# Gathering the experts' rows already transposed, two pairs at once from a three-part bfloat16 copy of h

## The reference, cut to what matters

```
def hier_moe(x, w_group, w_expert, w_gate, w_up, w_down):
    ...
    top_p, top_i = lax.top_k(jax.nn.softmax(e_logits, axis=-1), MOE_TOP_K)
    ...
    rows = xpad[row_tok].reshape(n_blocks, MOE_BLOCK, d)

    def expert_block(args):
        xb, e = args
        h = jax.nn.silu(xb @ w_gate[e]) * (xb @ w_up[e])
        return h @ w_down[e]

    yb = lax.map(expert_block, (rows, block_expert)).reshape(P, d)
    out = jax.ops.segment_sum(yb * row_w[:, None], row_tok, num_segments=T + 1)[:T]
```

## Time and profile before

| | us |
|---|---|
| median of 3 runs | 2106.32 |
| lowest, highest | 2104.14, 2111.51 |
| the profiled execution, its own time | 2105.5 |
| span of the profiled execution | 2103.7 |
| PE busy in the span | 2004.5 |
| DVE busy | 671.4 |
| ACT busy | 446.4 |

### The profile page before, as it was taken

The page is one execution under the profiler, slowest core; times in us unless marked ns, Lnnn a source line. Parts: engine busy times, 40 slices in busy tenths (PEclk is TensorE's granted clock), DMA queues, the critical chain, the costliest instruction groups (busy, mean ns, idle before and its releaser), DMA issues.

```text
span 2103.7 us, 20350 instructions
## 1 busy us (share of the span) xinstructions
PE 2004.5 (95%) x8337; PEld 1058.7 (50%) x8337; DVE 671.4 (32%) x1469; ACT 446.4 (21%) x961; POOL 61.0 (3%) x55
## 2 busy tenths in 40 slices
PE   9999999999999989978999999997779999989999
PEld 8888643333333334444333333332445656438873
DVE  3555331111111122224111111112224545424994
ACT  2222201011110101231110111101124433204770
POOL 0000000000000000000000000000000000000110
PEclk9999999999999999989999999999779999999999
DMA  9333338999999957214999999995411213231412
GB/s 387 126 121 121 117 144 354 423 426 428 428 427 428 428 227 326 80 40 180 387 424 426 426 427 428 428 428 230 168 49 40 121 40 120 81 120 40 200 57 84
DMA packets 40206, 522.46 MB, mean 248 GB/s; under 512 B 4384, under 2 KB 6944, under 8 KB 8368
## 3 DMA queue, kind: packets, MB, share of 16 engines
q1 hardware_dynamic: 38240, 514.52, 59.2%
q10 hardware_dynamic: 1872, 6.61, 0.8%
HBM read 520.06 MB, written 1.05 MB: 248 GB/s over the span
## 4 chain that ended last, share of the span: by engine, by line
PE 90%; DVE 5%; ACT 3%; DMA 1%; issue 1%; POOL 1%; SPq 0%; ACTq 0%; DVEq 0%
PE ps L194 33%; PE ps L602 21%; PE ps L624 11%; PE ps L634 6%; PE ps L573 5%; PE ps L589 1%; PE ps L1143 1%; PE ps L1014 1%; PE ps L982 1%; PE ps L966 1%; PE ps L869 1%; PE ps L987 1%; PE ps L509 1%; PE ps L610 1%; PE ps L522 1%
## 5 line engine op out<-in xcount | busy, mean ns | idle before, releaser
L602 PE MATMUL ps<-ring,work 128*64 128x512 f32 x2048 | 445.0, 592 | 0.7 <-issue 0.7
L194 PE MATMUL ps<-xT,ring 128*128 128x272 f32 (+1 forms) x1280 | 300.6, 394 | 2.1 <-DMA ring<-in_w_xz 1.8
L602 PEld LDWEIGHTS ps<-ring,work 128*64 128x64 f32 x2048 | 148.7, 137 | 290.3 <-issue 290.3
L194 PEld LDWEIGHTS ps<-xT,ring 128*128 128x128 f32 x1280 | 245.7, 193 | 48.7 <-issue 4.5
L624 PE MATMUL ps<-ring,work 128*64 128x512 f32 x1024 | 226.8, 595 | 1.4 <-ACT work L1321 1.4
L194 PE MATMUL ps<-ring,xT 128*128 128x256 f32 (+2 forms) x672 | 209.7, 471 | 3.8 <-DMA ring<-in_w_qkv 2.3
L194 PE MATMUL ps<-ring,big 128*128 128x512 f32 x448 | 199.9, 603 | 4.3 <-ACT ring L1558 1.8
L1813 DVE TENSOR_TENSOR work<-work,ps 128x512 f32<-128x512 f32 x32 | 22.0, 687 | 524.3 <-PE ps L602 524.3
L194 PEld LDWEIGHTS ps<-ring,xT 128*128 128x128 f32 x672 | 128.6, 194 | 80.0 <-issue 68.0
L194 PEld LDWEIGHTS ps<-ring,big 128*128 128x128 f32 x448 | 85.2, 193 | 110.5 <-issue 108.1
L624 PEld LDWEIGHTS ps<-ring,work 128*64 128x64 f32 x1024 | 70.7, 137 | 134.8 <-issue 127.9
(11 more groups left out here) (330 smaller groups left out, 1763.0 us busy)
## 6 DMA issues: line engine op xcount, KB each, us to landing
ring<-in_wg SPq DMA_DIRECT2D x64, 2048.0 KB, 14.5
ring<-in_wu SPq DMA_DIRECT2D x64, 2048.0 KB, 17.4
ring<-in_wd SPq DMA_DIRECT2D x64, 2048.0 KB, 13.2
ring<-in_w_odd SPq DMA_DIRECT2D x8, 2048.0 KB, 7.9
ring<-in_w_xz SPq DMA_DIRECT2D x7, 2048.0 KB, 17.5
ring<-in_w_qkv SPq DMA_DIRECT2D x6, 2048.0 KB, 19.5
ring<-in_w_bc SPq DMA_DIRECT2D x4, 2048.0 KB, 15.1
ring<-in_ssm_out SPq DMA_DIRECT2D x4, 2048.0 KB, 7.9
```

Source lines behind the costliest of these rows:

```text
L194: i = e.matmul(bout, lhs(k), rhs(k), start=start and k == ks[0], stop=stop and k == ks[-1])
L602: last = e.matmul(b[64 * j:64 * j + 64, :], xgT[:, p % 2, k, 64 * j:64 * j + 64], w[j][:, k, :], start=k == 0, stop=k == 7)
```

## The change

- The gather swaps its operands: h is now the stationary operand and S the moving one, so that the product comes out transposed. turn_x, `xgs` and its two copies are gone.
- Pairs 0 and 1 are gathered so in float32, each by itself: 16 matmuls of 128 columns.
- Pairs 2 to 15 are gathered two pairs at once. `hb` holds h as three bfloat16 parts: the rounded value, the rounded rest, and the rest of that. Sb, the 0/1 matrix for two pairs, is 256 wide and bfloat16. A piece s (2 to 15) is half of the 1024 rows of xgT for two pairs: 24 bfloat16 matmuls of 128 weight columns by 256, summed in float32. One piece is done for each pair, two pairs ahead; pair 1 has two pieces (s = 2 and 3).
- The three parts are made once in each layer: two casts on ScalarE and two subtractions on VectorE, of 2048 elements in each partition.
- In the loop the gather moves from before turn_h to after it. SW is turned in a function of its own (`tensor_turn_w`) just before down.
- The banks are fixed: ps0 for gate and the turned SW, ps1 for up and turn_h, ps2 and ps3 for gather and down. Down waits for the copies of the gather just before it; up waits for the copy of hT of the pair before; gate waits for the copy of the turned SW.

The core of the diff (the copies in `scalar_gathered` and `vector_gathered` write PSUM to xgT, one of each for a piece):

```diff
+        Sb = m(512).bitcast(BF16).rearrange("p (i t n) -> p i t n", i=2, t=2)
+        xgT, sg, hs, hT = m(2, 8, 256), m(512), m(512), m(4, 128)
+        rest = xgT[:, 1].rearrange("p k n -> p (k n)").rearrange("p (t n) -> p t n", t=2)
+        ys, hb = area(big, 0, (1024,)), big[:, 1024:4096].bitcast(BF16).rearrange("p (i t n) -> p i t n", i=3, t=2)
...
+        gate_b, up_b, swt_b, th_b, row_b = ps[0], ps[1], ps[0], ps[1], ps[2:4]
...
+        def tensor_gather(e, l, s):
+
+
+            e.wait_ge(*listed(l, s if s < 2 else s // 2 * 2))
+            if s == 2:
+                e.wait_ge(*hb1_in(l))
+                e.wait_ge(*hb2_in(l))
+                e.wait_ge(*hb3_in(l))
+            for i in range(2):
+                b = row_b[i]
+                if s:
+                    e.wait_ge(*(xg1 if i else xg0)(l, 0 if s == 1 else 2 if s == 3 else s - 1))
+                if s > 1:
+                    e.wait_ge(*(ys1 if i else ys0)(l, 0 if s < 4 else s - 3))
+                for k in range(4 if s < 2 else 2):
+                    if s < 2:
+                        o = b[:, k * 128:(k + 1) * 128]
+                        for t in range(2):
+                            last = e.matmul(o, h[:, t, (4 * i + k) * 128:(4 * i + k + 1) * 128], S[:, s, t, :],
+                                            start=t == 0, stop=t == 1)
+                    else:
+                        o, c = b[:, k * 256:(k + 1) * 256], (4 * (s % 2) + 2 * i + k) * 128
+                        for t, j in each(range(2), range(3)):
+                            last = e.matmul(o, hb[:, j, t, c:c + 128], Sb[:, s // 2 % 2, t, :],
+                                            start=t + j == 0, stop=t + j == 3)
+                last.then_inc(*gat_mm.up(l, s, i))
+
...
-        def tensor_turn_x(e, l, p):
-            for n in range(2):
-                e.wait_ge(*(xg0(l, p) if n == 0 else xg1(l, p)))
-                b = moe_bank(p - 1, TX0 + n)
-                for k in range(4):
-                    last = e.transpose(b[:, k * 128:(k + 1) * 128], xgs[:, (4 * n + k) * 128:(4 * n + k + 1) * 128],
-                                       ident)
-                last.then_inc(*tx_mm.up(l, p, n))
-
...
+            for s in ((p,) if p < 2 else (p // 2 * 2, p // 2 * 2 + 1)):
+                e.wait_ge(*xg0(l, s))
+                e.wait_ge(*xg1(l, s))
+            x = xgT[:, p // 2 % 2, :, 128 * (p % 2):128 * (p % 2) + 128]
+            for name, b, done in (("mg", gate_b, gate_mm), ("mu", up_b, up_mm)):
+                if name == "mg":
+                    e.wait_ge(*swt_in(l, p))
+                else:
+                    e.wait_ge(*(hT_in(l, p - 1) if p else flagged(l)))
...
-            if p + 1 < NE // 2:
-                e.wait_ge(*swt_in(l, p + 1))
...
+                b, s = row_b[n], 1 if p == 0 else min(p + 2, NE // 2 - 1)
+                e.wait_ge(*(xg1 if n else xg0)(l, s))
+                if p:
+                    e.wait_ge(*(ys1 if n else ys0)(l, p - 1))
...
             tensor_warm(e, ps[2], 6)
             tensor_gather(e, l, 0)
-            tensor_turn_x(e, l, 0)
+            e.matmul(ps[1][:, 0:32], ones[:, :], mk[:, 0, :], start=True, stop=False)
+            e.matmul(ps[1][:, 0:32], ones[:, :], mk[:, 1, :], start=False, stop=True).then_inc(*cnt_mm.up(l))
             e.wait_ge(*ranked(l))
-            e.matmul(b[:, 0:32], ones[:, :], mk[:, 0, :], start=True, stop=False)
-            e.matmul(b[:, 0:32], ones[:, :], mk[:, 1, :], start=False, stop=True).then_inc(*cnt_mm.up(l))
+            tensor_turn_w(e, l, 0)
             for p in P16:
                 tensor_hidden(e, l, p)
                 if p:
                     tensor_spread(e, l, p - 1)
+                if p == 1:
+                    tensor_gather(e, l, 2)
+                tensor_turn_h(e, l, p)
+                if p + 2 < NE // 2:
+                    tensor_gather(e, l, 1 if p == 0 else p + 2)
                 if p + 1 < NE // 2:
-                    tensor_gather(e, l, p + 1)
-                tensor_turn_h(e, l, p)
-                if p + 1 < NE // 2:
-                    tensor_turn_x(e, l, p + 1)
+                    tensor_turn_w(e, l, p + 1)
                 tensor_down(e, l, p)
...
+            e.copy(hb[:, 0], h[:, 0:2, :]).then_inc(*hb1_in.up(l))
             scalar_gathered(e, l, 0)
-            scalar_turned_x(e, l, 0)
+            scalar_turned_w(e, l, 0)
+            e.wait_ge(*rest_in(l))
+            e.copy(hb[:, 1], rest).then_inc(*hb2_in.up(l))
             for p in P16:
...
+        def vector_lists(e, l, s):
+
+            iota64 = R("iota")[:, 0:64]
+            if s > 4:
+                e.wait_ge(*gat_mm(l, s - 3, 1))
+            for j, t in each(range(2 if s < 2 else 4), range(2)):
+                x = 2 * s + j
+                o = S[:, s, t, 64 * j:64 * j + 64] if s < 2 else Sb[:, s // 2 % 2, t, 64 * j:64 * j + 64]
+                e.tensor_scalar(o, iota64, rk[:, t, x:x + 1], None, ALU.is_equal).then_inc(
+                    *(listed.up(l, s) if t and j == (1 if s < 2 else 3) else vs.up()))
+
...
+            vector_lists(e, l, 1)
+            vector_weights(e, l, 1)
+            e.wait_ge(*hb1_in(l))
+            e.tensor_tensor(rest, h[:, 0:2, :], hb[:, 0], ALU.subtract).then_inc(*rest_in.up(l))
+            vector_lists(e, l, 2)
+            e.wait_ge(*hb2_in(l))
+            e.wait_ge(*rest_in(l))
+            e.tensor_tensor(hb[:, 2], rest, hb[:, 1], ALU.subtract).then_inc(*hb3_in.up(l))
...
+                if p == 1:
+                    vector_gathered(e, l, 2)
+                if p + 2 < NE // 2:
+                    vector_gathered(e, l, 1 if p == 0 else p + 2)
+                    vector_weights(e, l, p + 2)
+                if p % 2 and p + 3 < NE // 2:
+                    vector_lists(e, l, p + 3)
```

More of the change, by code:

```diff
@@ L563, in tensor_router @@
             tensor_warm(e, idle, 20)
-        def tensor_gather(e, l, p):
-            e.wait_ge(*listed(l, p))
-            for n in range(2):
[L568 to L575, removed]
+        def tensor_gather(e, l, s):
[22 more added lines that the diff above has]
+                last.then_inc(*gat_mm.up(l, s, i))
@@ L576, in tensor_gather, with tensor_turn_w @@
+        def tensor_turn_w(e, l, p):
+            e.wait_ge(*weighted(l, p))
             if p:
                 e.wait_ge(*silu_in(l, p - 1))
-            e.wait_ge(*weighted(l, p))
-            b = moe_bank(p - 1, SWTB)
             for t in range(2):
-                last = e.transpose(b[:, t * 128:(t + 1) * 128], SW[:, p % 2, t, :], ident)
+                last = e.transpose(swt_b[:, t * 128:(t + 1) * 128], SW[:, p % 2, t, :], ident)
             last.then_inc(*swt_mm.up(l, p))
-        def tensor_turn_x(e, l, p):
-            for n in range(2):
-                e.wait_ge(*(xg0(l, p) if n == 0 else xg1(l, p)))
-                b = moe_bank(p - 1, TX0 + n)
-                for k in range(4):
-                    last = e.transpose(b[:, k * 128:(k + 1) * 128], xgs[:, (4 * n + k) * 128:(4 * n + k + 1) * 128],
-                                       ident)
-                last.then_inc(*tx_mm.up(l, p, n))
@@ L601, in tensor_hidden @@
                     for j in range(2):
-                        last = e.matmul(b[64 * j:64 * j + 64, :], xgT[:, p % 2, k, 64 * j:64 * j + 64], w[j][:, k, :],
+                        last = e.matmul(b[64 * j:64 * j + 64, :], x[:, k, 64 * j:64 * j + 64], w[j][:, k, :],
                                         start=k == 0, stop=k == 7)
@@ L1288, in scalar_mixed, with gathered, scalar_gathered, scalar_turned_w @@
             e.activation(s4[:, :, 4], s4[:, :, 3], ACT.Exp).then_inc(*e_exp.up(l))
[L1290 to L1294, removed]
+        def gathered(s, i):
+            if s < 2:
+                return xgT[:, 0, 4 * i:4 * i + 4, 128 * s:128 * s + 128]
+            k = 4 * (s % 2) + 2 * i
+            return xgT[:, s // 2 % 2, k:k + 2, :]
+        def scalar_gathered(e, l, s):
+            e.wait_ge(*gat_mm(l, s, 1))
+            e.copy(gathered(s, 1), row_b[1][:, :].rearrange("p (k n) -> p k n", k=4 if s < 2 else 2)
+                   ).then_inc(*xg1.up(l, s))
+        def scalar_turned_w(e, l, p):
             e.wait_ge(*swt_mm(l, p))
@@ L1297, in scalar_gathered @@
                 e.wait_ge(*spr_mm(l, p - 2))
[L1298 to L1304, removed]
+            e.copy(SWT[:, p % 2, :, :], swt_b[:, 0:256].rearrange("p (t n) -> p t n", t=2)).then_inc(*swt_in.up(l, p))
         def scalar_moe(e, l):
@@ L1320, in scalar_moe @@
                     e.wait_ge(*dn_mm(l, p - 1, 1))
[L1321 removed]
+                e.copy(hT, th_b[:, :].rearrange("p (f s) -> p f s", f=4)).then_inc(*hT_in.up(l, p))
+                if p + 2 < NE // 2:
+                    scalar_gathered(e, l, 1 if p == 0 else p + 2)
                 if p + 1 < NE // 2:
[L1323 removed]
+                    scalar_turned_w(e, l, p + 1)
                 e.wait_ge(*dn_mm(l, p, 1))
@@ L1326, in scalar_moe @@
                     e.wait_ge(*spr_mm(l, p - 1))
```

(2 more changed lines are left out.)

66 lines of the change are left out of this document (21 added, 45 removed).

## The result

The changed kernel takes 2096.19 us (median of five runs, 2093.76 to 2098.46) against 2106.32 before. The ratio is 0.995, with an interval of 0.9934 to 0.9967. The forecast was 2096.5. The profiled execution was the longest of the five, 2098.46, with a span of 2096.3, 7.4 less than before's span.

A forecast was written before the change was run, and what follows sets the result against it. PE and the expert loads were both taken as full, with loads setting the layer's end after the change. 2105.5 - 4.1 - 5.3 = 2096.1, plus 0.8 for the median, 2096.9; 2096.5 was taken, range 2088 to 2104.

The forecast's parts named there:

- The loads need as long for a pair as PE does: Mixture layers before the change: six 2 MiB loads take 29.5 us a pair, PE 29.34.
- The rival in which PE's saving counts in full: Both layers: PE's whole saving, 48 us, reaches the time, giving 2057; chance 0.03.
- The piece's cost, 0.114 a matmul, and a steady pair of 27.7: Gather on PE: 24 matmuls at 0.114 us make 2.75 a piece, taking a pair from 29.34 to 27.7.
- The slower rival: Gather pieces: weight loads stand in line with matmuls, a piece takes 5.3 us; down 11.4 late, 2128; chance 0.08.
- PE alone: down of pair 15 at 748.0: Layer 0's end without load waits: last down starts at 748.0, 24 us before 771.85.
- Waits of 1.8 us a pair from pair 7 on: Later pairs: PE waits 1.8 us a pair for mu, and the period goes to 29.5.
- The waits that cost nothing: Within a pair and at layer start: added waits for copies, products and h's parts stay hidden, costing 0.
- The chain of loads: Loads up to the last mu: 0.3 earlier start, plus md of pair 1's hole closed, 0.5 (layer 0) and 1.7 (layer 1).
- From the last mu to down, 11.74: Pair 15: after mu lands, up takes 6.92 us, then 4.82 more until down starts.
- the rival of the falling clock: Pair 15's new wait: clock falls to half, up loses 6.9 us a layer; 2110, or 2103 in one layer; chance 0.10.
- The sum, -4.1 and -5.3: Last down starts 4.1 us earlier in layer 0 and 5.3 in layer 1, passed on whole to the kernel's time.
- The end hardly depends on the unknown pace: Layer's end: loads set it unless each of 336 piece matmuls takes 0.059 us more, 0.173.

The follow-up runs named there:

- experiment 1: Kernel before the change, loading only the first half of each expert matrix in layer 1: 2106.3 us, ratio 1.0005.
- experiment 2: Changed kernel, loading only the first half of each expert matrix in layer 1: 2077.09 us, ratio 0.9862.
- experiment 8: Changed kernel with every matmul of a piece done twice (24 more per piece): 2130.89 us, ratio 1.0118.
- experiment 3: Changed kernel with all pairs gathered transposed in float32, one pair at a time, still two pairs ahead, no bfloat16 parts: 2099.56 us, ratio 0.9971.
- experiment 7: Changed kernel with 12 more bfloat16 matmuls in each piece: 2103.09 us, ratio 0.9986.
- experiment 4: Changed kernel with spread of the pair before moved between gate and up, and the gather's piece put before turn_h: 2094.47 us, ratio 0.9942.
- experiment 10: Changed kernel with every gather transposed in float32 without bfloat16 parts, one pair ahead instead of two: 2095.56 us, ratio 0.9946.
- experiment 9: Changed kernel with 12 more matmuls in each piece, only from piece 4 on: 2098.58 us, ratio 0.9963.

## Why the prediction was right, step by step

- **"The loads need as long for a pair as PE does", and "the loads forbid" PE's saving.** Shown by experiments 1, 2 and 8 and by the DMA share of 1.00. The rival in which PE's saving counts in full (2057) fell.
- **The piece's cost, 0.114 a matmul, and a steady pair of 27.7.** Measured 0.109 and 27.66. The slower rival, in which the weight loads (98 ns) stand in line, fell. By the Trainium skill (TensorE: Matmul & The Clock Gate, The mechanism) a load of weights overlaps matmuls only in another group of rows, and by the page's formulas a piece would then be an estimated 5.2 us; the trace has 2.62, and the trace decides. The same section also lets a load into a background weight buffer go ahead, which the trace does not contradict; no run here can tell whether that is what happens.
- **PE alone: down of pair 15 at 748.0.** Counted from the start of gate, forecast there at 314.6, that is 433.4; experiment 2 has 432.5.
- **Waits of 1.8 us a pair from pair 7 on.** In layer 0 there are nine, 15.8 us in all, the first at 518.88. Most are 1.5, two are 2.7, and the period is 29.4.
- **The waits that cost nothing.** So it was: the parts of h were done at 323.3, forecast before 325, and no wait of over 0.9 us but for loads stands in either layer.
- **Gate 0.3 earlier.** From the first gather to gate it was 5.08 for 5.75: 0.67. The transposes of SW lie beneath the first copies more than was allowed for.
- **The chain of loads.** This term was sized too small. The last mu was to land 0.8 earlier in layer 0 and 2.0 in layer 1. From the first gather it landed at 444.5 (733.07 + 22.1 - 310.72) against 447.7 before, and at 444.6 (1410.39 + 22.1 - 987.86) against 447.7: 3.2 and 3.1 earlier. Little of it is the start: the first waiting load was issued 0.67 earlier, but landed only 0.3 earlier in layer 0 and 0.2 in layer 1. The late landings are the main part: up to the last mu, gaps of over 5.3 us add up, above 4.9 each, to 2.9 and 3.4, where before they came to 6.0 and 5.9. Both holes at md of pair 1 closed (gaps of 5.5 and 7.7 before, 4.9 now). The prediction had the second at 1.7 over its pace of 4.96, taking the load ahead to land as in layer 0, and it was 2.7. The other late landings are four and four before (up to 6.6) and two and four after (up to 6.4); why they came is not known, so a part of the gain in layer 0 may be chance.
- **From the last mu to down, 11.74.** Measured 768.85 - 755.19 = 13.66. 1.7 of the excess is the clock, 0.1 the time to up's start. This is the rival of the falling clock in a smaller form: it was priced at 6.9 us a layer and came at 1.7 and 1.5. The prediction named a clock of 0.50 within a layer as a sign that it is wrong, and that sign came: its sum had no term for the clock.
- **The sum, -4.1 and -5.3.** Measured -4.6 and -4.6. The chain gave 2.4 us (layer 0) and 1.1 us (layer 1) more than forecast and the clock took 1.7 and 1.5 back, so part of the agreement is two errors of opposite sign. That the median came within 0.3 us of the forecast is luck beyond that: the profiled executions differ by 7.0 us and the medians by 10.1.
- **"The end hardly depends on the unknown pace".** This step was wrong in what it left out. Experiments 3 and 7 stayed under its bound of 0.059 us more for each matmul, and lost 3.4 and 7 us. Slack at the end of a layer says nothing of pair 1, where the load of md waits for down while few loads are in the queue.

What stays open: why the clock falls at some waits of 2.4 to 2.7 us and not at others, why some loads land late that were issued in time, what lengthens the stretch between the layers, and whether experiment 4 is really quicker than the changed kernel.

## What to carry to other kernels

Before an engine is made quicker, divide the stage's bytes by the rate that its full window shows. Here that gave 29.5 us a pair beside PE's 29.34, so of the 24 us that PE saves in a layer (456.99 - 432.46) the layer gave back only 4 (456.99 - 453.05). When a stage is bound by a ring of loads, its slack is not one number: each instruction between two loads that wait for slots, above all in the first pairs, must be looked at for when its load is issued, since a hole there stayed in the chain to the layer's end (experiment 3 against 10). And the simplest part alone (experiment 10) is worth running beside the whole change; here it gave the same time.

## What the runs showed of the hardware

- Twenty-four bfloat16 matmuls of 256 columns, each with new 128x128 weights, run at 0.109 us apiece (2.62 us in all), with weight loads of 98 ns wholly beneath them.
- In the layers the granted clock went to 0.50 twelve times in the eleven traces of the changed kernel and its variants, each time at a wait of PE for a load: eleven times for 3.4 us at waits of 2.4 to 2.7 us, once for 6.8 at one of 3.7 (experiment 9). A fall of 3.4 costs up to 1.7 us (8.78 for 7.10). Eight other waits of 2.4 to 2.7 us had none, among them both of experiment 3.
- Loads of 2 MiB in a full queue land 4.9 us apart (six in 755.19 - 725.81 = 29.38 us). Now and then one lands later, by up to 1.9 us (6.8 behind the one ahead of it in experiment 9), though it was issued in time.
